# High weights against both halves of the input in one product of 512 columns, for the output, up and down projections

## The reference

```python
# layers 0 and 1
mixed = (sigmoid(ga) * o_attn + sigmoid(gm) * o_ssm) @ w_out[l]        # 1024 -> 1024
x = x + g1 * mixed
h = rms_norm(x, norm2_g[l]) * (1.0 + sc2) + sh2
u = causal_dwconv(h @ w_up[l], ffn_conv_w[l], ffn_conv_b[l])           # 1024 -> 5632, 3 taps
val, gate = split(u, 2)
x = x + g2 * ((silu(gate) * val) @ w_down[l])                          # 2816 -> 1024
# block 3
x = x + y @ w_out                                                      # 1024 -> 1024
x = x + square(relu(rms_norm_2(x, mlp_norm) @ w_up)) @ w_down          # 1024 -> 4096 -> 1024
```

## Time and profile before

| | us |
|---|---|
| median of 3 runs | 1779.45 (1767.55 to 1781.22) |
| profiled execution, whole | 1764.97 |
| its span | 1763.0 |
| PE busy | 1623.5 (92%) |
| POOL busy | 1252.3 (71%) |
| DVE busy, ACT busy | 863.1 each (49%) |

### The profile page before, as it was taken

How to read it: one execution, slowest core, us unless ns; L and a number is a source line. 1 busy time by engine, 2 the same in 40 slices (tenths; PEclk the granted TensorE clock), 3 DMA queues, 4 the chain that set the end, 5 groups by cost and what they waited for, 6 DMA issues and landing times.

```text
span 1763.0 us, 33656 instructions
## 1 busy us (share of the span) xinstructions
PE 1623.5 (92%) x13130; PEld 1570.7 (89%) x13130; DVE 863.1 (49%) x1762; ACT 863.1 (49%) x1416; POOL 1252.3 (71%) x948
## 2 busy tenths in 40 slices
PE   5999999989989999999999989989998986589999
PEld 5989998989989998989998989989998984479999
DVE  6677676365436742667677365434421254432200
ACT  2554545554456644555545554356654442335532
POOL 2678966655769998678966655769998890049996
PEclk7999999989989999999999989999999996599999
DMA  8446744556446666456744556446656650036664
GB/s 309 139 151 205 238 156 134 167 194 201 144 143 228 219 236 207 144 150 203 240 149 146 158 199 207 136 129 191 189 182 180 227 166 12 1 96 183 189 191 132
DMA packets 85516, 302.72 MB, mean 172 GB/s; under 512 B 9840, under 2 KB 12528, under 8 KB 85104
## 3 DMA queue, kind: packets, MB, share of 16 engines
q1 hardware_dynamic: 85360, 300.59, 53.3%
HBM read 299.50 MB, written 1.05 MB: 170 GB/s over the span
## 4 chain that ended last, share of the span: by engine, by line
PE 70%; DVE 8%; POOL 7%; issue 6%; ACT 3%; DVEq 3%; DMA 2%; SPq 1%; ACTq 0%; POOLq 0%
PE gemm_bank L1498 58%; POOL w_lo L391 7%; PE turn_bank L1658 2%; ACT w_hi L409 2%; DVE conv L751 1%; DVEq L1212 1%; DVE idx_score L751 1%; PE outp_bank L1801 1%; PE turn_bank L1811 1%; PE outp_bank L1693 1%; PE turn_bank L1606 1%; DVE probs L948 1%; DMA ada_first<-in_w_ada 1%; PE outp_bank L1625 1%; PE outp_bank L1695 1%
## 5 line engine op out<-in xcount | busy, mean ns | idle before, releaser
L391 POOL TENSOR_TENSOR w_lo<-w_raw,w_hi 128x512 fp32r<-128x512 f32 x944 | 1252.1, 1356 | 499.5 <-ACT w_hi L409 478.1
L409 ACT ACTIVATE w_hi<-w_raw 128x1024 fp32r<-128x1024 f32 x472 | 492.4, 1046 | 655.2 <-PE gemm_bank L1498 605.1
L1498 PE MATMUL gemm_bank<-h_hi,w_hi 128*128 128x256 f32 x2112 | 606.7, 287 | 30.1 <-issue 13.0
L1498 PE MATMUL gemm_bank<-h_lo,w_hi 128*128 128x256 f32 x2112 | 597.3, 283 | 0.0
L1498 PE MATMUL gemm_bank<-h_hi,w_lo 128*128 128x256 f32 x2112 | 596.7, 283 | 0.0
L1498 PEld LDWEIGHTS gemm_bank<-h_hi,w_hi 128*128 128x128 f32 x2112 | 405.5, 192 | 41.0 <-issue 19.8
L1498 PEld LDWEIGHTS gemm_bank<-h_lo,w_hi 128*128 128x128 f32 x2112 | 405.7, 192 | 0.2
L1498 PEld LDWEIGHTS gemm_bank<-h_hi,w_lo 128*128 128x128 f32 x2112 | 405.2, 192 | 0.0
L751 DVE SCALAR_TENSOR_TENSOR conv<-gemm_bank,params_sb,conv 128x255 f32<-128x255 f32 (+1 forms) x320 | 139.6, 478 | 165.7 <-ACT conv L686 112.7
L1498 PE MATMUL gemm_bank<-w_hi,h_hi 128*128 128x256 f32 (+2 forms) x704 | 206.2, 293 | 10.3 <-issue 10.0
L1498 PE MATMUL gemm_bank<-w_lo,h_hi 128*128 128x256 f32 (+2 forms) x704 | 201.2, 286 | 0.0
(11 more groups left out here) (290 smaller groups left out, 2179.5 us busy)
## 6 DMA issues: line engine op xcount, KB each, us to landing
w_raw<-in_stream SPq DMA_DIRECT2D x458, 512.0 KB, 3.7
ada_w<-in_w_ada SPq DMA_DIRECT2D x80, 512.0 KB, 4.7
ada_first<-in_w_ada SPq DMA_DIRECT2D x16, 512.0 KB, 12.3
w_raw<-in_stream SPq DMA_DIRECT2D x8, 256.0 KB, 3.0
alibi_sb<-in_alibi SPq DMA_DIRECT2D x1, 1920.0 KB, 7.2
rows_sb<-in_rows SPq DMA_DIRECT2D x1, 1536.0 KB, 10.6
residual<-in_x_t SPq DMA_DIRECT2D x1, 1024.0 KB, 7.3
out_x<-residual SPq DMA_DIRECT2D x4, 256.0 KB, 4.6
```

The source lines that it names most:

```text
L391: ins = nc.gpsimd.tensor_tensor(w_lo[:, s, e], w_raw[:, s, e], w_hi[:, s, e].bitcast(f32), ALU.subtract)
L409: A(w_hi[:, s, 0:n], w_raw[:, s, 0:n], ACT.Copy).then_inc(hi_ready, 1)
L1498: ins = M(o, a, b, start=first and i == 0, stop=last and i == len(passes) - 1, skip_group_check=True)
```

## The change

In the units named by `WIDE` and `WIDE2` (output units 0 to 2 of 4, all up units, down units 0 to 2 of 4, in all three layers) the high weights take both parts of the input in one product: the moving operand is `x[:, :, kt, :]`, high part and low part, 2 x 256 = 512 columns, and the result fills a whole bank. So a unit needs two banks, one for each column half: `gemm[b]` and `S.bank[b]`, a bank of the pair that the attention scores use. The low weights still take the high part alone, 256 columns, and add to the lower half of the bank. Afterwards the two halves of each bank have to be added. In up units ACT copies the upper halves to `work` (`crossing`), DVE adds them to the lower halves in PSUM (`join`), and ACT's first pass waits for that. In output and down units `add_to_x` adds both halves to the residual one after the other. The high and low tensors are laid out side by side (`H`, `OT`, `YB`, `F`, `F2`), `mod_ps` moves to another bank, and PE waits once for the last scores before the output projection (`scores_read`). The last output unit and the last down unit, and all other projections, stay as they were.

```diff
+WIDE = ((U_OUT, U_OUT + 3), (U_UP, U_DN), (U_DN, U_DN + 3))
+WIDE2 = ((V_OUT, V_OUT + 3), (V_UP, V_DN), (V_DN, V_DN + 3))
...
+        def gemm_banks(l, o):
+            b = gemm_use(l, o)[0]
+            return (gemm[b], S.bank[b]) if wide(l, o) else (gemm[b],)
...
+        def crossing(l, i, j):
+
+            return work[:, 2 * j + i % 2, SEQ:2 * SEQ]
... (ACT, up units of layers 0 and 1)
-                    bank_u, _ = unit_done(l, u)
+                    unit_done(l, u)
+                    banks = gemm_banks(l, u)
+                    if i >= 2:
+                        act.wait_ge(up_joined, joined(l, i - 2))
+                    for j in range(2):
+                        a = A(crossing(l, i, j), banks[j][:, SEQ:2 * SEQ], ACT.Copy)
+                    a.then_inc(up_cross, 1)
+                    if i >= 1:
+                        up_gate(i - 1)
                     if i >= 2:
                         act.wait_ge(up_prod, n - 1)
+                    act.wait_ge(up_joined, joined(l, i))
                     for j in range(2):
                         t = j * FT + i
-                        a = A(conv[:, i % 2, j * SEQ:(j + 1) * SEQ], bank_u[:, j * SEQ:(j + 1) * SEQ], ACT.Identity,
+                        a = A(conv[:, i % 2, j * SEQ:(j + 1) * SEQ], banks[j][:, 0:SEQ], ACT.Identity,
                               scale=col("ffnw", 2 * 2 * FT + t), bias=col("ffnb", t))
                     a.then_inc(up_first, 1)
-                    if i >= 1:
-                        up_gate(i - 1)
... (ACT, up units of block 3)
+                for j in range(2):
+                    a = A(crossing(l, i, j), banks[j][:, SEQ:2 * SEQ], ACT.Copy)
+                a.then_inc(up_cross, 1)
                 if i >= 1:
                     up2_high(i - 1)
+                act.wait_ge(up_joined, joined(l, i))
+                for j in range(2):
+                    a = A(conv[:, i % 2, j * SEQ:(j + 1) * SEQ], banks[j][:, 0:SEQ], ACT.Relu)
+                a.then_inc(up_first, 1)
... (DVE)
+            def join(l, o, i):
+
+                banks = gemm_banks(l, o)
+                dve.wait_ge(up_cross, joined(l, i))
+                for j in range(2):
+                    ins = V.tensor_tensor(banks[j][:, 0:SEQ], banks[j][:, 0:SEQ], crossing(l, i, j), ALU.add)
+                ins.then_inc(up_joined, 1)
+                dve.drain()
+
             def add_to_x(l, o, j, g_col):
 
                 b, k = gemm_use(l, o)
-                for i in range(2):
-                    g = 1.0 if g_col is None else g_col[:, 2 * j + i:2 * j + i + 1]
-                    ins = stt(XT[:, 2 * j + i, :], gemm[b][:, i * SEQ:(i + 1) * SEQ], g, XT[:, 2 * j + i, :], ALU.mult, ALU.add)
+                banks = gemm_banks(l, o)
+                for half in range(len(banks)):
+                    if half:
+                        dve.drain()
+                    for i in range(2):
+                        g = 1.0 if g_col is None else g_col[:, 2 * j + i:2 * j + i + 1]
+                        src = banks[i][:, half * SEQ:(half + 1) * SEQ] if wide(l, o) else banks[0][:, i * SEQ:(i + 1) * SEQ]
+                        ins = stt(XT[:, 2 * j + i, :], src, g, XT[:, 2 * j + i, :], ALU.mult, ALU.add)
                 ins.then_inc(gemm_read[b], 1)
... (DVE, up units of layers 0 and 1; in block 3 up2_low moves in the same way)
+                    join(l, u, i)
+                    if i >= 1:
+                        up_product(i - 1)
                     dve.wait_ge(up_first, l * FT + i + 1)
...
                     ins.then_inc(gemm_read[b], 1)
-                    if i >= 1:
-                        up_product(i - 1)
                     if i >= 2:
                         up_low(i - 2)
... (PE)
+            def feature_passes(g, banks, x, j, kt, k):
...
+                if len(banks) > 1:
+                    o = banks[j]
+                    return [(o[:], wh, x[:, :, kt, :]), (o[:, 0:SEQ], wl, x[:, 0, kt, :])]
+                o = banks[0][:, j * SEQ:(j + 1) * SEQ]
+                return [(o, wh, x[:, 0, kt, :]), (o, wh, x[:, 1, kt, :]), (o, wl, x[:, 0, kt, :])]
```

More of the change, by code:

```diff
@@ L230, in build @@
         O = Banks(bank, sem, "outp", 22)
-        mod_ps = S.bank[1][:, CW:CW + 2 * KT]
+        mod_ps = T.bank[0][:, CW:CW + 2 * KT]
         shift_ps = T.bank[1][:, 0:KT]
@@ new lines, in feature_tile, with token_tile, feature_chunk @@
+            def feature_tile(g, banks, x, kt, k, first, last):
+                for j in range(2):
+                    ins = products(feature_passes(g, banks, x, j, kt, k), first and (j == 0 or len(banks) > 1), last)
+                return ins
+            def token_tile(g, banks, x, kt, k, first, last):
+                for j in range(2):
+                    ins = products(token_passes(g, banks, x, j, kt, k), first and j == 0, last)
+                return ins
+            def feature_chunk(g, banks, x, k0, first, last):
+                weights(g)
+                kts = chunk_words(*layer_chunk(g)) // 256
+                for j in range(2):
+                    for k in range(kts):
+                        ins = products(feature_passes(g, banks, x, j, k0 + k, k), first and k == 0 and (j == 0 or len(banks) > 1),
+                                       last and k == kts - 1)
+                ins.then_inc(chunk_done, 1)
@@ L1558, in token_chunk @@
+            def token_chunk(g, banks, x, k0, first, last):
+                weights(g)
+                for j in range(2):
                     for k in range(4):
-                        passes += [(o, xh[:, k0 + k, c], wh[:, k, :]), (o, xh[:, k0 + k, c], wl[:, k, :]),
-                                   (o, xl[:, k0 + k, c], wh[:, k, :])]
-                products(passes, first, last).then_inc(chunk_done, 1)
-            def part(l, u, p, chunk, xh, xl, n=2, k0=None):
+                        ins = products(token_passes(g, banks, x, j, k0 + k, k), first and k == 0 and j == 0, last and k == 3)
+                ins.then_inc(chunk_done, 1)
@@ L1565, in part @@
+            def part(l, u, p, chunk, x, n=2, k0=None):
                 b, k = gemm_use(l, u)
@@ L1591, in arrived, with scores_read @@
                 pe.wait_ge(pair.read[b], k + 1)
+            def scores_read(l):
+                for h in range(HEADS - 2, HEADS):
+                    arrived(S, l, (S_AT if l < DEPTH else S2_AT) + h)
             def first_sum(v, out, signal, more=False):
@@ L1650, in from_norm @@
                 pe.wait_ge(h_ready, n + KT)
[L1651 to L1652 removed]
+                part(l, u, 1, chunk, H)
+                part(l, u + 1, 1, chunk, H)
             def turn(l, i, blocks):
```

166 lines of the change are left out of this document (75 added, 91 removed).

## The result

| | before | after |
|---|---|---|
| median | 1774.32 us (1767.22 to 1781.22, 20 runs) | 1787.13 us (1780.01 to 1792.98, 20 runs) |
| span of the profiled execution | 1763.0 | 1785.4 |
| mean granted clock | 0.946 | 0.943 |

The ratio is 1.0075, with a 95% interval of 1.0061 to 1.009: 12.8 us more, where 10 us less was forecast.

What follows compares the result with a forecast made beforehand. PE, busy 92% of the span, was taken as the bound, POOL next. 3.4 + 2.4 + 2.6 + 0.5 + (1.2 - 1.8) - 1.0 + 2.7 = 10 us saved, from 1779.45 to 1769; own range 1761 to 1776, 80% range 1757 to 1791.

Steps and rivals of the forecast that it cites:

- I take 215.8: Wide product of 512 columns: 215.8 ns, read from the square sums; 332.7 with the low product, 17.9 saved from 350.5.
- the 6 ns between 104 and 256 columns: Product price: 104 columns cost 6 ns less than 256, so mostly the weight load sets the pace and wider products could hide it.
- Rival A: Twice the columns cost twice the time, 233.7 ns per product, leaving only the price: 9 us slower, 1789; chance 0.10.
- Where PE alone bounds: Block 3's down 3.4 us, layer 1's down 2.4 and output 2.6: all of the product saving comes through there.
- 5.75 forecast: Up units, layers 0 and 1: time from a unit's end until its bank is back, 5.75 us, from 3.96.
- the 1.04 taken: Layer 1's up: the product of the unit before, now ahead of the taps, takes 1.04 us, the middle of observed times.
- The forecast 5.55 a unit: Layer 1's steady up units: period 5.55 us set by POOL, against 5.61; 20 units give 1.2 us.
- Rival B: The chain decides in up units from 5.90 us on; at 6.74 the period is 6.03: 10 us slower, 1790; chance 0.16.
- The starts: Start of up stages: PE waits 2.93 us instead of 1.16, losing 1.8 in layer 1, 1.0 in layer 0; block 3 1.9.
- POOL is over a chunk ahead with them: ACT's high parts of the next chunk come about 1.6 us later, covered by POOL's lead in a ring of four.
- POOL gets ahead meanwhile: Layer 0's up start: POOL gains a lead during PE's wait and bounds afterwards, so 1.0 us is lost there, not 1.8.
- delay the next join by 0.4: Layer 0's up: `ada` after every second unit ends at 7.9, the next join is due at 7.5; steady units gain nothing.

Runs made afterwards that it cites:

- the ruler: The changed kernel with seven stretches of 48 products, 512 to 64 columns wide, appended behind its last down unit; 1828.5 us.
- up01_narrow: The changed kernel with the up units of layers 0 and 1 as before the change, output, down and block 3's up still wide; 1771.55 us, ratio 0.9994.
- early_copies: The changed kernel with ACT's copies of the upper halves in up units ahead of the high part of the next chunk; 1771.92 us, ratio 1.0002.
- the second execution: Trace of the changed kernel with products appended behind its last down unit, unchanged up to there; layer 0 takes 210.4 us, layer 1 207.7.
- from_two: The changed kernel with the first two up units of layers 0 and 1 narrow as before the change, units 2 to 21 wide; 1778.88 us, ratio 1.0025.
- two_early: from_two with ACT's copies ahead of the high part of the last chunk, and ACT's first pass likewise ahead in the XBC units; 1765.09 us, ratio 0.9942.
- all_early: early_product plus ACT's first pass ahead of the high part of the last chunk in the XBC units; 1778.55 us, ratio 1.0034.
- early_product: The changed kernel with ACT's copies ahead of the next chunk's high part and the up product behind DVE's taps; 1779.02 us, ratio 1.0045.
- product_behind: The changed kernel with the product of the unit before behind DVE's four taps again in up units of layers 0 and 1; 1788.76 us, ratio 1.0097.

## Why the prediction was wrong

**The product (the failed step).** "I take 215.8" for 512 columns. It is 231 to 235, and the pair 347 instead of 332.7: 3.5 ns saved per triple instead of 17.9. On the 1560 products this is 5.5 us in place of 28 before any price. The nearest row misled in two ways: the square sums are of unrounded data, two records a product, and I read their 215.8 as 512 cycles; and the 6 ns between 104 and 256 columns were taken for a floor that goes on, where the ruler has its knee between 192 and 256. Rival A had the argument right (256 columns are 106.7 of 116.85 at 2.4 GHz) and got 0.10. Its price, 233.7, is within the measured 231 to 235. That its time, 1789, is within 2 us of the median is in part luck: it starts from 1779.45, 5 us above the median of twenty runs of before, and adds 9 where 12.8 was measured; the restart and the clock below are not in it. Of the two figures that the Trainium skill gives in "TensorE: Matmul & The Clock Gate", section "Back-to-back issue gap", the isolated 512/2.4 + 2.5 (215.8 by its formula) is 15 to 19 ns under what the trace shows for this rounded type, and the sustained 131 ns at 512 columns is 100 or more under it. The prediction's "agrees on 512 cycles (215.8)" rested on records of 256 columns of the unrounded type, not on a product of 512 columns.

**Where PE alone bounds.** Block 3's down, layer 1's down and the output units were to give 8.4 us. At 3.5 ns a triple it is 1.6, too little for any run here to show: up01_narrow, which has all of them, is at 0.9994. The mechanism was right (no waits came in, joins in block 3 took 0.43 as costed), its size was the product's.

**Layer 1's chain.** 5.75 forecast, 5.84 measured. Copies (0.65 for the pair, from 0.76) were cheaper, joins right (0.43), and the product at 1.42 to 1.49, in the units whose chain PE waits for, costlier than the 1.04 taken. What I had not costed is the restart: PE's first eight products behind a wait take 1.67 instead of 1.39. About 0.11 of the 0.28 is a longer first step; the rest is that the last product ends later than its place in the stream says, 0.28 after its start and not 0.12. It is so in before too, 3.07 instead of 2.80 for 24, in a row that follows those of the earlier trace rows and that I did not use:

```profile
1181.94 3.07 PE gemm_bank L1498 x24
```

With 5.56 for PE, 5.84 + 5.56 + 0.28 = 11.68 for two units, 11.68 to 11.74 measured. The forecast 5.55 a unit needed a fast PE to pay for the chain. POOL was not the bound here: it waits 1.06 to 1.12 and 0.30 in two units, where it had 0.25 a unit. Rival B's point of 5.90, from which the chain decides, was worked out with 5.32 for PE; with 5.56 and the restart of 0.28 it lies at 2 x 5.61 - 5.84 = 5.38, which the forecast's own chain of 5.75 exceeds. Early copies bring it below, and the waits end.

**The starts.** Forecast were 1.8 more in layer 1 (1.0 in layer 0) and 1.9 in block 3. The waits came out at 2.7 and 3.0, from 1.2, and 1.3, from none. What was missing is the granted clock: in the profiled execution 2.7 us in layer 0 and 1.6 in layer 1 were lost at 1.2 GHz, in the second execution nothing in layer 0 and 1.3 in layer 1. How often it falls in the other runs is not shown. from_two, which takes the longer wait away, got two thirds of the loss back (1.0075 to 1.0025, each within 0.2%), 7.5 us by the stages; it does not part the wait from the clock.

**Layer 0.** "POOL is over a chunk ahead with them" was to cover ACT's late high parts, and in the steady units it did: POOL has one gap of 0.23 in 85 us. The wrong step is the start, for which I took 1.0 because "POOL gets ahead meanwhile". POOL did not get ahead, it waited. PE was late (the wait of 3.0) and slow (the clock), so it freed its slots late; ACT stood 3.7 us for one before it could make the next high part, and POOL 4.5 us for ACT. By the table the start costs 5.8 of the layer's 8.2 us, and 2.8 of 4.9 in the second execution, with the clock at 1.00. The units behind it cost 2.0 more, 1.6 of them in gaps where up passes into down. A POOL that is full makes up nothing, so what the start loses stays lost. from_two and two_early, whose first two units are narrow, have the start back (49.3 and 48.9), and early copies bring the units back to 97.5.

**`ada`.** I had it delay the next join by 0.4. In after it ends just before the join (DVE goes from one to the other without a gap); moving the product behind the taps made that real, and cost 5 us in layer 0.

## What to carry to other kernels

Before betting on wider products, measure their price in a stretch with no waits: one kernel with 48 of each size showed that 256 columns already sit on the slope. When a chain that gives a buffer back is within a few tenths of what covers it, cost its restart and the clock behind its longest wait as well; each was larger here than the saving per unit. Ask also what the engine next to the bound waits for while PE stands still: if it is full afterwards, it never makes that up. Read a stage in a second execution of the same kernel before believing 3 us of it. And look for what stands in the chain without belonging there: moving 1 us of unrelated work on ACT behind the copies gave back more than the change had lost in layer 1.

## What the runs showed of the hardware

- Products of the rounded 4-byte type: 0.45 ns per column from 256 to 512, 0.11 us at the least, each with its own weight load.
- Waits of 1.2 us at the two stage starts kept the granted clock at 1.00 behind them in all five kernels that have them, and so did those of 1.7 in layer 1 in three kernels. Behind longer ones it fell in some executions and not in others: of three waits of 2.0 in layer 0, two (early_copies, all_early, to 0.76 and 0.57 in a stretch of 4 us, not early_product); of three of 2.7 in layer 1, two (after to 0.66, the second execution to 0.57, not product_behind); of three of 3.0 and 3.1 in layer 0, two (after and product_behind to 0.50, not the second execution). The Trainium skill, in "TensorE: Matmul & The Clock Gate", section "HAM oscillation — how this bites in real kernels", tells of waits that cost the product behind them their clock; the trace agrees that they can, and shows it not to be certain from the length alone.
- A stream of 48 products of 64 columns was slower than one of 128 (0.137 against 0.111), at a granted clock of 0.85 and 0.88 in its stretches, though PE was busy without a gap.
- DVE's multiply of two SBUF operands (`up_product`) takes 0.43 us when no subtraction of POOL runs at its start. Otherwise it ends about 0.29 after the end of the one that runs, in nearly all of the 42 units of the change where one does: 0.48 to 1.57 in before's layer 0. Here the subtraction ends at 1220.10 and the product at 1220.39:

```profile
1218.78 1.32 POOL L417 TENSOR_TENSOR w_lo<-w_raw,w_hi 128x512 fp32r<-128x512 f32 x1
1218.90 1.49 DVE L1401 TENSOR_TENSOR outp_bank<-work,conv 128x256 f32<-128x256 f32 x1 [0.16 <-issue]
```

- DVE's joins, with one operand in PSUM, stay at 0.41 to 0.43 in both layers.
